# Fill blocks in two pairs of PSUM banks, block ends moved off stage ends, and dense products that begin with two plain chunks

## What is computed

```python
def even_layer(x, ...):
    h = rms_norm_2(x, norm_g) @ w_in
    y = concatenate([gdn_branch(...), diff_attention(...), memory_attention(...)], axis=-1)
    return x + y @ w_out

def odd_layer(x, ...):
    h = rms_norm_2(x, norm_g) @ w_in
    y = concatenate([window_attention(...), mla_attention(...), memory_attention(...)], axis=-1)
    return x + y @ w_out
```

## Time and profile before

| | |
|---|---|
| median of 3 runs | 2779.04 us (2777.98 to 2779.92) |
| the profiled execution, its own time | 2780.15 us |
| its span, first to last instruction | 2778.4 us |
| busy: TensorE, VectorE, ScalarE | 2604.9 (94%), 1315.8 (47%), 939.1 us (34%) |
| mean granted clock of TensorE | 0.988 |
| dense products of L358 to L360, x608 + x256 each | 711 + 303 us |
| plain products of L671 | 557 us |

### The profile page before, as it was taken

One profiled execution on the slowest core, in us unless ns is written; L12 is line 12 of the kernel. 1 busy time (PEld: TensorE's weight loads), 2 busy tenths in 40 slices (PEclk: granted clock), 3 DMA queues, 4 the chain that ended last, 5 costly groups with the idle time before them and its releaser, 6 DMA issues. The chain is left out here.

```text
span 2778.4 us, 37907 instructions
## 1 busy us (share of the span) xinstructions
PE 2604.9 (94%) x14224; PEld 1746.0 (63%) x14224; DVE 1315.8 (47%) x2541; ACT 939.1 (34%) x1672; POOL 116.8 (4%) x133
## 2 busy tenths in 40 slices
PE   8999999999888889999998999999899999998999
PEld 7984555887444444447975776855446855774557
DVE  5654694665311112226764545563525543454435
ACT  5544122444121212224534323432214422432224
POOL 0001111020011110010000000000010000001000
PEclk9999999999999999999999999999999999999999
DMA  7754333554399999994432014543322542443224
GB/s 302 218 208 159 136 141 136 184 203 152 138 422 422 422 422 422 403 358 159 169 128 77 32 47 159 191 180 112 127 110 100 195 170 91 170 156 106 84 106 152
DMA packets 80741, 532.78 MB, mean 192 GB/s; under 512 B 9136, under 2 KB 13616, under 8 KB 19152
## 3 DMA queue, kind: packets, MB, share of 16 engines
q1 hardware_dynamic: 76560, 517.65, 49.0%
q0 software_dynamic: 3456, 11.02, 1.6%
q10 hardware_dynamic: 576, 2.10, 0.2%
HBM read 522.86 MB, written 7.86 MB: 191 GB/s over the span
## 5 line engine op out<-in xcount | busy, mean ns | idle before, releaser
L410 DVE TENSOR_TENSOR split_wl<-ring,split_wh 128x512 fp32r<-128x512 f32 x432 | 298.4, 699 | 214.1 <-ACT split_wh L384 212.4
L384 ACT ACTIVATE split_wh<-ring 128x512 fp32r<-128x512 f32 x432 | 270.6, 631 | 272.7 <-PE ps L360 270.8
L2172 PE MATMUL ps<-ring,yT 128*64 128x256 f32 x2048 | 247.9, 387 | 52.4 <-DMA ring<-in_weights 48.3
L671 PE MATMUL ps<-ring,xT 128*128 128x512 f32 x576 | 262.4, 609 | 20.3 <-ACT odm_qg L2988 5.1
L465 PE MATMUL ps<-features_xh,features_wh 128*128 128x256 f32 x832 | 236.8, 285 | 1.5 <-DVE features_wl L456 1.5
L358 PE MATMUL ps<-split_wh,split_xh 128*128 128x512 f32 x608 | 238.0, 391 | 0.0
L360 PE MATMUL ps<-split_wh,split_xl 128*128 128x512 f32 x608 | 236.6, 389 | 0.0
L359 PE MATMUL ps<-split_wl,split_xh 128*128 128x512 f32 x608 | 236.5, 389 | 0.0
L2172 PEld LDWEIGHTS ps<-ring,yT 128*64 128x64 f32 x2048 | 138.1, 137 | 155.2 <-DMA ring<-in_weights 91.0
L467 PE MATMUL ps<-features_xh,features_wl 128*128 128x256 f32 x832 | 235.4, 283 | 0.0
L671 PE MATMUL ps<-ring,yT 128*128 128x512 f32 x448 | 208.2, 618 | 18.4 <-PEq L2658 7.5
(11 more groups left out here) (643 smaller groups left out, 4001.1 us busy)
## 6 DMA issues: line engine op xcount, KB each, us to landing
ring<-in_weights SPq DMA_DIRECT2D x468, 1024.0 KB, 5.1
x_res<-in_x SPq DMA_DIRECT2D x1, 2048.0 KB, 7.5
yT<-in_mem SPq DMA_DIRECT2D x1, 2048.0 KB, 15.8
rel_skew<-lru_feat POOLq DMA_DIRECT2D x1, 2048.0 KB, 49.7
mem_features<-yT ACTq DMA_DIRECT2D x4, 512.0 KB, 6.5
s_wb<-in_s_bc POOLq DMA_DIRECT2D x4, 512.0 KB, 4.1
s_wc<-in_s_bc POOLq DMA_DIRECT2D x4, 512.0 KB, 4.0
gate_bias<-in_gate_bias POOLq DMA_DIRECT2D x8, 256.0 KB, 3.9
```

The source lines that it names most:

```text
L384: nc.scalar.activation(wh[:, c % deep, :], raw(unit, turn, c), ACT.Copy).then_inc(w_high.sem, 1)
L410: last = nc.vector.tensor_tensor(wl[:, c % deep, :], raw(unit, turn, c), wh[:, c % deep, :], ALU.subtract)
L671: last = nc.tensor.matmul(k.ps[:, 6 + t, :], x[:, kc, t * P:(t + 1) * P], k.ring[:, slot, c * BLK:(c + 1) * BLK], start=kc == 0, stop=kc = ...
L2172: last = nc.tensor.matmul(k.ps[s * WIN:(s + 1) * WIN, p, 0:FF], window[:, p, kc, :], k.ring[:, slot, at:at + FF], start=kc == 0, stop=kc = ...
```

## The change

`gemm_tokens`: the first `LEAD = 2` chunks of the first block are multiplied plainly, straight from x and the ring; the five dummies are gone. The low and high parts of x for chunks 0 and 1 are made at the end of the first block, for the blocks behind it. VectorE frees the first unit only after `led`.

`Fill` gets a pair of banks for each block (`pairs`, 3 is banks 6 and 7, 1 is banks 2 and 3, 2 is banks 4 and 5), and waits for the last block in the same pair. `fill_x` takes the place of `add_to_x` in fills: VectorE's add of the second half no longer waits for ScalarE and counts for `fill_v`; the add of the copied half follows.

The step counts: `attention` gets `first` steps ahead of the first transposes, norms get more, turns fewer. The lambda block gets two steps; the window branch's load block is folded into its `head_norm` (`bring`). The dummies behind the even layer's memory branch are dropped (`busy=0`); those at the end of the differential branch go to bank 7 (`idle=7`).

```diff
@@ gemm_tokens, TensorE, ScalarE, VectorE
+                            if first and kc < LEAD:
+                                if c == 0:
+                                    unit_wait(k, pe, base, 0, 2 * upb)
+                                for t in range(NT):
+                                    last = nc.tensor.matmul(k.ps[:, t, :], x[:, kc, t * P:(t + 1) * P], raw(base, 0, c), start=kc == 0, stop=False)
+                                if kc == LEAD - 1:
+                                    last.then_inc(led.sem, 1)
+                                continue
...
+                    if first and pieces:
+                        pe.wait_ge(x_low.sem, x_low.at(len(pieces) - 1))
-
-                keep_busy(k, pe, 5, 5)
                 each_block_late(pe, blocks, upb, body)
...
+                    if first and pieces:
+                        nc.scalar.activation(xh[:, 0:LEAD, :], x[:, 0:LEAD, :], ACT.Copy).then_inc(x_high.sem, 1)
...
+                        if first and g == 0:
+                            dve.wait_ge(led.sem, led.at(0))
                         dve.drain().then_inc(k.unit_used, 1)
@@ fill_x, new
+    def finish_act(act, b, j):
+        return nc.scalar.activation(copied[:, b % 2, :], k.ps[:, 2 * j, :], ACT.Copy)
+
+    def finish_dve(dve, b, j):
+        return nc.vector.tensor_tensor(k.x[:, 1, ds(b * BLK, BLK)], k.ps[:, 2 * j + 1, :], k.x[:, 1, ds(b * BLK, BLK)], ALU.add)
+
+    def add_copied(b):
+        return nc.vector.tensor_tensor(k.x[:, 0, ds(b * BLK, BLK)], copied[:, b % 2, :], k.x[:, 0, ds(b * BLK, BLK)], ALU.add)
@@ Fill
-            if kc == 0:
-                pe.wait_ge(fill_a.sem, fill_a.at(n - 1))
-                pe.wait_ge(fill_v.sem, fill_v.at(n - 1))
+            same = [m for m in range(n) if self.pairs[m] == self.pairs[n]]
+            if kc == 0 and same:
+                pe.wait_ge(fill_a.sem, fill_a.at(same[-1]))
+                pe.wait_ge(fill_v.sem, fill_v.at(same[-1]))
...
-            dve.wait_ge(fill_a.sem, fill_a.at(n))
-            self.blocks[n][3][1](dve, self.blocks[n][2], 3).then_inc(fill_v.sem, 1)
+            _, _, b, (_, finish, *rest) = self.blocks[n]
+            finish(dve, b, self.pairs[n]).then_inc(fill_v.sem, 1)
+            for add in rest:
+                dve.wait_ge(fill_a.sem, fill_a.at(n))
+                add(b)
@@ attention, TensorE (ScalarE: store_act before begin; VectorE: store_dve behind begin(0))
+                if first:
+                    fill.multiply(pe, first)
                 each_turn(pe, begin, body)
@@ memory_attention, twice: norm, attention, end
-                  fill=fill, steps=8, loaded=loaded)
+                  fill=fill, steps=10, loaded=loaded)
-              fill=fill, steps=(3, 3, 1, 1), bring=bring, beside=beside)
+              fill=fill, first=2, steps=[(3, 2, 1, 0), (3, 1, 0, 1)], bring=bring, beside=beside)
@@ even: last 12 -> 13 steps, busy=0; odd: last 8 -> 9 steps
+        fill = Fill(..., pairs=[3, 1, 3, 1, 3])
+        fill = Fill(..., pairs=[3, 1, 3, 1])
@@ diff_branch: lambda block, norm, attention, last norm
+            fill.multiply(pe, 2)
+                pairs=[3, 3, 3, 3, 3, 2])
-    head_norm(..., fill=fill, steps=8)
+    head_norm(..., fill=fill, steps=9)
-              fill=fill, steps=(4, 4, 2, 2), turned=...)
+              fill=fill, first=1, steps=[(4, 2, 2, 2), (4, 2, 2, 2), (4, 4, 1, 1), (4, 2, 2, 2)], turned=...)
-              fill=fill, steps=8, turn=Turned(..., HEADS, 7))
+              fill=fill, steps=12, turn=Turned(..., HEADS, 10, idle=7))
@@ swa_branch
+        fill = Fill(k, (k.xT, KC, 2, tokens_to(k, mla_gate)), (k.xT, KC, 1, tokens_to(k, pq)), pairs=[3, 1, 3])
-        wait_loads(k, reach, bias, fill=fill, steps=4)
+        wait_loads(k, reach, bias, fill=fill, steps=2)
-                      ..., fill=fill, steps=[(3, 3, 1, 1), (3, 3, 1, 1) if g == 0 else (2, 2, 0, 0)])
+                      ..., fill=fill, first=3, steps=[(3, 3, 1, 0), (3, 2, 0, 1) if g == 0 else (2, 1, 0, 1)])
@@ mla_branch
+        fill = Fill(k, (k.xT, KC, 2, tokens_to(k, qg)), (features[:, :, :], KC, 1, tokens_to(k, values)), pairs=[1, 3, 3])
-                  steps=[(3, 3, 1, 1), (2, 2, 1, 0), (2, 2, 1, 0), (2, 2, 0, 0)], turned=...)
+                  first=2, steps=[(3, 2, 1, 0), (2, 2, 1, 0), (2, 2, 1, 0), (2, 1, 0, 1)], turned=...)
```

More of the change, by code:

```diff
@@ L311, in gemm_tokens, with step @@
     evac_a, evac_v = k.ev("evac_a"), k.ev("evac_v")
-    x_high, x_low, w_high, w_low, w_used = (k.ev(n) for n in ("x_high", "x_low", "w_high", "w_low", "w_used"))
+    x_high, x_low, w_high, w_low, w_used, led = (k.ev(n) for n in ("x_high", "x_low", "w_high", "w_low", "w_used", "led"))
     per = 2 * chunks
+    def step(j, kc):
+        return j * chunks + kc - LEAD
     with ExitStack() as scope:
@@ L393, in finish @@
                 def finish(turn, j):
-                    dve.wait_ge(w_used.sem, w_used.at((j + 1) * chunks - 1, turn, per))
+                    dve.wait_ge(w_used.sem, w_used.at(step(j + 1, -1), turn, per))
                     if dve_after_act:
@@ L419, in gemm_tokens @@
     k.used += blocks * upb
-    steps = blocks * chunks
-    k.ended(evac_a=blocks, evac_v=blocks, x_high=len(pieces), x_low=len(pieces), w_high=steps, w_low=steps, w_used=steps)
+    steps = blocks * chunks - LEAD
+    k.ended(evac_a=blocks, evac_v=blocks, x_high=len(pieces), x_low=len(pieces), w_high=steps, w_low=steps, w_used=steps, led=1)
 class FeatureSplit:
@@ L2664, in _ @@
                 if fill:
-                    fill.load(sp, sum(sum(s) for s in by_turn))
+                    fill.load(sp, first + sum(sum(s) for s in by_turn))
             @block.gpsimd
@@ L2762, in body @@
                     store(i, 3)
+                if first:
+                    fill.store_act(act, first)
                 each_turn(act, begin, body)
@@ L2838, in body @@
                     store(i, 3)
-                each_turn(dve, begin, body)
+                each_turn(dve, begin, body, (lambda: fill.store_dve(dve, first)) if first else None)
     k.ended(dve_a=heads, dve_b=heads, dve_d=heads, act_a=heads, act_b=heads, act_c=heads, pe_a=heads, pe_b=heads, pe_c=heads, pe_d=heads)
@@ L3842, in _ @@
             load(k, sp, kv[:, :, :], k.ev_kv)
+            fill.load(sp, 2)
+        @block.tensor
+        def _(pe):
+            fill.multiply(pe, 2)
         @block.vector
@@ L3903, in swa_branch, with bring @@
         reach = k.sb(scope, "swa_reach", [P, NT, SEQ])
[L3904 to L3911 removed]
+        fill = Fill(k, (k.xT, KC, 2, tokens_to(k, mla_gate)), (k.xT, KC, 1, tokens_to(k, pq)), pairs=[3, 1, 3])
+        def bring(sp):
+            sp.wait_ge(k.kv_stored, 48)
+            load_bias(k, sp, bias)
+            load(k, sp, reach[:, :, :], k.dram["window"])
         free = k.yT[:, 8:16, :].rearrange("p a b -> p (a b)")
         nk = n + kv_heads * P
[L3915 to L3916 removed]
+        head_norm(k, [ps[:, t, 0:nk].rearrange("p (h w) -> p h w", w=P) for t in range(NT)], P, free, fill=fill, steps=12, bring=bring)
+        wait_loads(k, reach, bias, fill=fill, steps=2)
         for g in range(kv_heads):
@@ L3921, in swa_branch @@
                       float(P) ** -0.5, bias_at=lambda h, t: bias[:, t, ds(h + g * per, 1), :].rearrange("p a b -> p (a b)"),
[L3922 removed]
+                      sink_at=lambda h: k.rows[:, ds(h + (ROW_AT["sink"][0] + g * per), 1)], fill=fill, first=3,
+                      steps=[(3, 3, 1, 0), (3, 2, 0, 1) if g == 0 else (2, 1, 0, 1)])
         gate = nk + kv_heads * P
@@ L3935, in mla_branch @@
         kr_w = free[:, 0:KC * rope].rearrange("p (c n) -> p c n", c=KC)
-        gemm_tokens(k, None, 3, KC // UNIT_KC, *store_tokens(k, pq, BLK), whole=k.layer, ahead=lambda sp: load(k, sp, kr_w, k.dram["mla_kr_w"]))
+        gemm_tokens(k, k.xT, 3, KC // UNIT_KC, *store_tokens(k, pq, BLK), whole=k.layer, ahead=lambda sp: load(k, sp, kr_w, k.dram["mla_kr_w"]))
         kr = k.sb(scope, "mla_kr", [P, NT, rope])
```

105 lines of the change are left out of this document (62 added, 43 removed).

## The result

The changed kernel takes **2704.93 us** (median of 4 runs, 2704.46 to 2713.76), the kernel before 2779.48 us in the same comparison (4 runs, 2777.98 to 2782.16): ratio 0.9744, 95% interval 0.972 to 0.9768. That is 74.5 us, where my sum had 63.9. Run once more in a later comparison it took 2709.32 us (2705.55 to 2710.59) against 2780.73, ratio 0.9742 (0.9726 to 0.9758).

A forecast was written before the change was run, and what follows sets the result against it. TensorE, busy 94% of the span, bounds the kernel, so time comes only from its work, waits and low clock. 11.6 + 5.8 + 11.5 + 9.6 + 7.6 + 2.05 + 17.0 - 1.3 = 63.9 us gives 2716 us, range 2704 to 2736.

The forecast's parts named there:

- Part 1: Nine dense product starts: five dummies dropped and two chunks done plainly save 1.29 us each, 11.6 us in all.
- Rival 3: Product starts give nothing because chunk 2 or chunk 4 waits for VectorE: 2728 us, chance 0.05.
- Part 2: Lambda block filled and window branch's load block folded into its norm: TensorE's two empty blocks go, 5.8 us.
- Part 5: Stage ends: no block ends where an attention ends, 7.6 us; dummies behind the even memory branch go, 2.05 us.
- Part 3: Attention starts: fill steps cover VectorE's staging, so waits of 16.1 us shrink to 4.6, a gain of 11.5 us.
- Part 4: Fill-block evictions: ScalarE and VectorE run together, alternate bank pairs; waits go except 2.3 us in differential turn 0, 9.6 us.
- Part 6: Twelve half-clock windows behind waits go at 1.56 us each, one may return: 17.0 us; the skill's rule would remove 7.8.
- Part 7: Added waits in attention turns left without a fill step between turned probabilities and their product, or with fewer: -1.3 us.
- rival 1: The clock doesn't come back: twelve windows at 1.2 GHz remain behind hand-overs and short waits, 2733 us, chance 0.10.
- rival 2: In-order VectorE: differential turn 0's 2.3 us wait shows up at eight other block ends, 18.4 us, 2734; chance 0.09.
- rival 4: Slower: 24 fill steps taken from attention turns were needed as cover, costing 91.7 us in waits and clock, 2808; chance 0.02.
- rival 5: Changing banks costs clock: a window at each of eleven changes of pair, 17.2 us, 2733; chance 0.01.

The follow-up runs named there:

- run 7: Changed kernel with the one to three fill steps ahead of each attention's first transposes moved behind the first scores: 2716.43 us, ratio 0.9779.
- Run 3: Changed kernel with VectorE again waiting for ScalarE's copy at a fill block's end before making its own: 2718.14 us, ratio 0.9792.
- run 4: Kernel before with the parallel eviction alone, for fill blocks that are copied out: 2771.64 us, ratio 0.9982.
- run 6: Changed kernel with fill steps at their old places and the even memory branch's dummies back, keeping two bank pairs, parallel evictions and new product starts: 2731.48 us, ratio 0.9833.
- run 10: The changed kernel once more, unaltered, as the mark for other runs: 2709.32 us.
- run 11: Changed kernel with the differential attention's first turn at (3, 3, 2, 2) fill steps instead of (4, 2, 2, 2): 2713.44 us, ratio 0.976.
- run 1: Kernel before with the new product start alone (two plain chunks, no dummies, all nine dense products): 2767.8 us, ratio 0.996.
- run 5: Changed kernel with all fill blocks in one pair of banks, 6 and 7: 2740.83 us, ratio 0.9872.
- run 8: Kernel of run 7 with five dummies added ahead of the first transposes of each attention: 2724.0 us.

## Why the prediction was right, and where it was not

**What bounds it, and where.** Right for 67 of 75.8 us: they came from TensorE's waits, the stretches at half clock and its own dummies, at the places named. The branches brought 53.7 where parts 2 to 7 have 52.3. That the measured 2704.93 still lies in the range, 0.9 us above its lower end, is partly luck: that end was reached with 2.6 us more for the clock, leftover waits that close and 3 us of pace, and what filled it was a stretch that the sum doesn't have.

**Part 1, product starts.** The mechanism held, and so did the price of two plain chunks, 3.49 us. 1.29 each was forecast, 1.43 to 1.58 measured within the product. Two things were left out, and they cancel: before, the first split chunk behind the dummies took 1.55 us, 0.19 more than the others, and went with them; and the hand-over ahead of a product grew by some 0.15 us (0.49 in the timeline above, 0.35 in the earlier trace rows). 1.44 - 0.15 = 1.29 at the second product. Rival 3 is out: no wait for `w_low` at a start.

**Parts 2 and 5, empty blocks and stage ends.** The hand-overs out of attentions are six of 2.8 us together, the longest 0.8, where I had five of 0.35: right in kind, 1 us too low. The dummies behind the even memory branch are gone; no run has them alone.

**Part 3, starts of attentions.** 11.5 us forecast; taking the cover away (run 7) costs 10, and its trace has 10.2 us more of waits. Size right, though the clock's share (below) was too high in what I expected of that run. Of the waits that I left at the starts, 1.4, 1.3 and 0.8, the trace has 1.24, 1.12 and 0.81; the 1.4 doesn't follow from the two figures beside it (17.34 - 15.7 = 1.6).

**Part 4, evictions: the step that failed.** The waits went as forecast, and turn 0 of the differential attention waits 1.48 + 0.22 us where I had 2.3, for the reason given:

```profile
1856.01 0.69 DVE L3064 COPY evm_qg<-ps 128x512 f32<-128x512 f32 x1 [2.14 <-PE ps L727]
...
1856.62 0.41 DVE L2923 TENSOR_TENSOR att_q<-diff_q,rows_sb 128x256 f32<-128x256 f32 x1
...
1857.45 0.44 PE L2753 MATMUL ps<-ident_sb,att_q 128*128 128x128 f32 x2 [1.48 <-DVEq L2851]
```

But the part looked at evictions only in the branches. The sentence "the first two run together" holds for every fill block, and four lie between products 3 and 4. Worth: 9.1 us there, of them 3.2 in hand-overs by the trace (0.81, 0.70, 0.71, 0.15, 0.15, 0.10, and 0.55 at product 4's start) and two half-clock stretches that went, 3.1; some 3 are spread in small pieces, 0.9 of them two waits for loads near 784 us. Run 3 shows the line that brings the hand-overs. That the two half-clock stretches hang on it is not shown: the one near 1645 us came back in run 3, but it is also there in runs 4, 6, 10 and 11, with parallel evictions, and absent from run 1, without them. So some 6 us of this stretch stay open, half of them the clock's. I also didn't see how much the second pair carries. I credited it with the waits of before (12.2 us), while at the new places its absence costs 36 (run 5).

**Part 6, the clock.** All twelve half-clock windows of the branches (stretches of 3.4 us) are gone and none came up anew; the 17.0 has a slip in it, 18.7 - 1.56 is 17.1. The page TensorE: Matmul & The Clock Gate of the Trainium skill lists, in its section "Loop structure matters more than you think", a VectorE copy out of PSUM as not breaking TensorE's warmth, in a loop whose next products follow immediately. Where the next products had to wait for the copy, the traces have it otherwise: the clock fell behind the 2.23 us wait of the earlier trace rows, and in run 11 behind 2.62 us. The sum of 56 that the prediction works out by that sentence is 18 us short of what was measured, the forecast 10.6. But "a wait, then a window" is not a rule. In run 6 the six starts wait 2.44, 2.51, 1.90, 1.89, 2.10 and 2.50 us, and this is the granted clock right behind them (columns as in run 8):

```profile
1848.30:1851.70 3.40, 3.40 (x16) 2.63 (x18) 0.76 (x2) 1.92 (x3) 0.00 (x0) 0.51 0.47 200
1995.10:1998.50 3.40, 3.18 (x11) 2.71 (x11) 0.46 (x2) 2.48 (x3) 0.00 (x0) 0.51 1.03 359
2257.90:2261.30 3.40, 3.40 (x9) 2.64 (x8) 1.69 (x5) 1.72 (x2) 0.00 (x0) 0.51 0.13 55
2298.50:2301.90 3.40, 3.17 (x17) 2.57 (x18) 1.55 (x5) 1.19 (x2) 0.00 (x0) 1.00 0.63 265
2494.80:2498.20 3.40, 3.14 (x20) 2.25 (x20) 1.21 (x5) 1.99 (x4) 0.00 (x0) 1.00 0.61 258
2599.20:2602.60 3.40, 3.40 (x13) 2.65 (x12) 0.50 (x2) 2.17 (x3) 0.00 (x0) 0.50 0.35 149
```

1.90 us at the third was followed by half clock, 1.89 at the fourth was not. Over all fourteen traces, from product 4 on, waits of 1.89 to 2.62 us had half clock within 2 us of their end in 24 of 44 cases, waits of 3.15 us and more in 18 of 18, and waits of 1.30 to 1.81 us in 1 of 27 (run 8). The kernel before had already shown it: its two window attentions start behind the same 2.60 us wait, and only the second lost the clock, which is how I took a price from the earlier trace rows. My expectation of run 7 (six windows behind six waits) is the form in which this was wrong. What decides between two like waits stays open.

**Part 7.** The wait for the turned probabilities is 1.0 us over four turns, the forecast was 1.3.

**Rivals.** 1 is out for the changed kernel: behind the leftover waits (at most 1.48 us) the clock stayed in both of its profiles, though run 8 shows that it can fall behind the same one. 2 is out (five waits on staging, 2.5 us). A relative of it, which I hadn't listed, comes once the next block has the same banks (runs 5 and 11): the fill, not the transposes, then waits for VectorE. 4 is out: no turn waits for exponentials. 5 is out: eleven changes of banks and no window. The Trainium skill's "A second HAM failure mode: psum-queue depth-cycling" (TensorE: Matmul & The Clock Gate) tells of a bf16 kernel that changes banks in each iteration; here 8 or 16 steps lie between two changes, and no run changes banks more often.

## What to carry to other kernels

Moving the end of background work away from a stage's end and giving it a second pair of banks are one change: away from the stage's end the eviction stands behind the foreground's work in ScalarE's and VectorE's order, and only other banks let TensorE go on. When a diff edits a helper, list every caller before pricing it; the helper's callers outside the named places made the largest miss here. Dummies ahead of a hand-over cost time as soon as they end behind what the hand-over waits for: compare the two at each place. Here two to four fewer won time at eight of twelve places and nothing at four, and no run shows that the ones dropped had kept the clock up.

## What the hardware showed that was not expected

Two waits of TensorE as alike as 1.90 and 1.89 us were followed by clocks of 0.51 and 1.00, so for waits near 2 us a window's 1.56 us can only be forecast as a share of cases, 24 of 44 here. A profile of the same kernel can differ by three such windows from the next (the two of the changed kernel), in places that no edit touched. Runs of the same kernel on one chip differ by as much as a few windows: the kernel before took 2773.0 us at a mean clock of 0.990 and 2784.95 at 0.985. And where kinds of products meet, a start alone misleads: the first split product starts 3.11 us behind the first of four plain ones, but the next one only 0.63 us later instead of 0.23, so that the two fill steps' 3.49 us come out in full.
